# Reading cached value pages four at a time in every second unit, in a one-core decoder-layer kernel

## The chip, the core and the metric

The kernel runs on one core of a Trainium2 chip. The metric is device time in microseconds, from one launch; the median of three runs of the kernel before is 2697.33 us (2696.64 to 2697.48).

## The reference, cut to what matters

One decoder layer is computed for a prompt of 256 tokens and for 8 samples of one token each (264 rows in all), in float32: a half-step FFN, a combined projection into three branches, the gates, an output projection, and a second half-step FFN. Two branches read caches of the samples, and these are what the change is about:

```python
k_past = cache_k[l][page_table].reshape(DB, past_len, A_HEADS, A_DH)   # 8 samples x 8 pages of 128 x 1024 f32
v_past = cache_v[l][page_table].reshape(DB, past_len, A_HEADS, A_DH)
...
o = einsum('bhqsj,bhqsjd->bqhd', p_sel, vs) + einsum('bhqj,bhjd->bqhd', p_own, v_own)   # attention over pages (MoBA)
...
s = einsum('bqhd,bmhd->bhqm', q, mk) * (M_DH ** -0.5)                   # attention over 256 memory tokens
return einsum('bhqm,bmhd->bqhd', softmax(s), mv)
```

A sample has 8 key pages and 8 value pages (512 KB each), and 2 key blocks and 2 value blocks of memory (512 KB each).

## The kernel before, in words

**The main stream.** Every weight matrix goes through TensorE in units. `sp_mid_unit` (SyncE) loads a block of weights into one of four places of `raw` (1 MB, or 512 KB for the short units); ACT copies it rounded into `splitH` (`act_split`, L487), DVE makes the remainder `splitL` (`dve_split`, L493), and PE runs three matmuls for each pair of tiles (`pe_unit`, L533 to L535) against the 264 columns. A long unit has 48 matmuls, a short one 24. The middle of the kernel is one loop of 176 units, T = 0 to 175, that every engine writes out in full. In the stretch of the gates, T = 64 to 127, the units with T % 4 of 0 and 1 are long (gate weights) and those with T % 4 of 2 and 3 are short (branch weights); T = 128 to 143 are long again.

**The side work.** Everything else is hung behind units by number: after unit T, PE runs `pe_side(T)`, ACT runs `act_side(T)` after its split for unit T + 2, and DVE runs `dve_side(T)` after its split for unit T + 2. The prompt's own attention over eight heads is one such side work (`pe_heads` with `KA`): from T = 109 to 132 nearly every unit has a score product, a transposition or an output product of it (T = 130 has none, and T = 108 has none).

**The ring.** Pages of keys and values of both branches pass through five places of 512 KB, `ring` (RING = 5). `uses()` sorts all reads by the unit in which they end, PE's reads ahead of DVE's within a unit; the n-th page of that list takes place n % 5, and so the place of the page five before it. POOL issues the loads in that order (`sp_page`, L1630), each after a wait for `page_used` of its place; `LOAD_AT` sets only where in POOL's program the load stands (about six units behind the use that frees the place), so it is the wait that paces it. Key pages are read by DVE (`dve_half_page`, L1674), half a page at a time; `KEY_AT` says how many halves stand in which unit. At T = 83, 86, 89 and 92 two halves stand: the second of one page and the first of the next. Value pages are read by PE as the moving operand of small matmuls with 8 columns of probabilities as weights:

```python
1974:        s = page_there(pe, ("V", k, g))
1975:        for j in range(4):
1976:            last = nc.tensor.matmul(PS[32 * j:32 * j + A_HEADS, 4, 0:2 * P], DA["L"][:, k, g, :],
...
1978:        last.then_inc(page_used[s], 1)
```

(`pe_value_page`; `pe_mem_values` at L1964 does the same for the two blocks of a sample's memory.) When the eight pages of a sample have been read, ACT copies the PSUM rows out (`act_row_copy`), PE transposes them ahead of the next sample's first page (`pe_row_turn`, L1510), and DVE takes the diagonal out (`dve_past_row_out`).

**The two lists of the change.** `MEM_AT` gives the unit in which each sample's memory values are read, `VALUE_AT` how many value pages each unit reads. The steps of PE, ACT and DVE all follow these lists, and so do the ring's order and POOL's loads. Before, memory values stand in T = 83, 84, 86, 87, 89, 90, 92 and 93, two blocks each; value pages stand in T = 108 to 131 as 3, 2, 1, 2 by T % 4, and two each in T = 132 to 139.

Of the kernel before, what the change touches and what calls it, by code (L numbers as in the profile page):

```python
# [83 lines left out]
def build(nc, d, o, sem, PS, block):  # L84
# [1418 lines left out]
    def pe_row_turn(pe, n):  # L1503

        pe.wait_ge(row_sb, n + 1)
        wait_count(pe, row_out, n)
        if n == MEM_ROWS:
            pe.wait_ge(a_lo, M_HEADS)
        for et in range(2):
            last = nc.tensor.transpose(PS[:, turn_bank(n), et * P:(et + 1) * P], row_tile(n)[:, n % 2, et, :], ident[:, :])  # L1510
        last.then_inc(row_turned, 1)

    def dve_rows_out(dve, n, out):

        dve.wait_ge(row_turned, n + 1)
        for et in range(2):
            rows = PS[:, turn_bank(n), et * P:(et + 1) * P].rearrange("p (h c) -> p h c", h=4)
            last = nc.vector.tensor_copy(out[:, et:BT:2, :], rows[:, :, 0:DEC])
        last.then_inc(row_out, 1)
# [59 lines left out]
    assert sum(KEY_AT.values()) == 2 * len(KEYS)  # L1579
    MEM_AT = (83, 84, 86, 87, 89, 90, 92, 93)  # L1580
    VALUES = [("V", k, g) for k in range(DEC) for g in range(NPAGES)]
    VALUE_AT = {**{T: (3, 2, 1, 2)[T % 4] for T in range(108, 132)}, **{T: 2 for T in range(132, 140)}}
    assert sum(VALUE_AT.values()) == len(VALUES)

    def uses():

        at_slot, n = [], 0
        for T in sorted(KEY_AT):
            for _ in range(KEY_AT[T]):
                n += 1  # L1590
                if n % 2 == 0:
                    at_slot.append((T, 1, KEYS[n // 2 - 1]))
        for b, T in enumerate(MEM_AT):
            at_slot += [(T, 0, ("MV", b, g)) for g in range(2)]
        v = 0
        for T in sorted(VALUE_AT):
            for _ in range(VALUE_AT[T]):
                at_slot.append((T, 0, VALUES[v]))
# [33 lines left out]
    def page_read(eng, page):  # L1632

        n = PAGE_NO[page]
        eng.wait_ge(page_used[n % RING], n // RING + 1)
# [277 lines left out]
    def act_exps(act, K):  # L1913

        act.wait_ge(d_logit, K.q + 1)
        last = nc.scalar.activation(K.t["L"][:, :, :, :], K.t["L"][:, :, :, :], ACT.Exp)
        if K is DKA:
            last = nc.scalar.activation(K.t["eo"][:, :, :], K.t["om"][:, :, :], ACT.Exp)
        last.then_inc(d_exp, 1)
# [16 lines left out]
    def dve_probs(dve, link, K):  # L1936

        t = K.t
        dve.wait_ge(sum_ps, K.q + 1)
        tot = PS[:, sum_bank(K), 2 * P:2 * P + DEC * K.heads].rearrange("p (b h) -> p b h", b=DEC)  # L1940
        if K is DKA:
            link(nc.vector.tensor_tensor(t["rd"][:, :, :], tot, t["eo"][:, :, :], ALU.add))
        else:
            link(nc.vector.tensor_copy(t["rd"][:, :, :], tot))
        link(nc.vector.reciprocal(t["x1"][:, :, :], t["rd"][:, :, :]))
        for g in range(K.pages):
            last = nc.vector.tensor_tensor(t["L"][:, :, g, :], t["L"][:, :, g, :], t["x1"][:, :, :], ALU.mult)
        if K is DKM:
            link(last)
            w = K.pages * K.heads  # L1950
            last = nc.vector.tensor_copy(t["one"][:, :].rearrange("p (b c) -> p b c", b=DEC)[:, :, 0:DEC * w:DEC],
                                         t["L"][:, :, :, :].rearrange("p b g h -> p b (g h)"))
        last.then_inc(d_prob, 1)

    def pe_mem_values(pe, b):

        if b == 0:
            pe.wait_ge(d_prob, 1)
            pe.wait_ge(row_sb, MEM_ROWS)
        for g in range(2):  # L1960
            s = page_there(pe, ("MV", b, g))
            for h in range(M_HEADS):
                c0 = DEC * (M_HEADS * (2 * b + g) + h)
                last = nc.tensor.matmul(PS[32 * h:32 * h + DEC, 4, 0:M_DH], DM["one"][:, c0:c0 + DEC],  # L1964
                                        ring[:, s, h * M_DH:(h + 1) * M_DH], start=b == 0 and g == 0,
                                        stop=b == DEC - 1 and g == 1)
            last.then_inc(page_used[s], 1)
# [132 lines left out]
    def pe_side(pe, T, values):  # L2100
# [24 lines left out]
        for b in range(DEC):  # L2125
            if T == MEM_AT[b]:
                pe_mem_values(pe, b)
        if T == MEM_AT[DEC - 1] + 1:
            pe_row_turn(pe, MEM_ROWS)
# [4 lines left out]
        pe_heads(pe, KA, T, MOBA, 3, 5)  # L2134
        for _ in range(VALUE_AT.get(T, 0)):
            k, g = values // NPAGES, values % NPAGES
# [8 lines left out]
    def pe_heads(pe, K, T, t0, pitch, lag):  # L2145

        for h in range(K.heads):
            t = t0 + pitch * h
            if T == t:
                att_scores(pe, K, h)  # L2150
            if T == t + 4:
                att_turn(pe, K, h)
            if T == t + lag:
                att_out(pe, K, h)
# [12 lines left out]
    def dve_heads(dve, link, K, T, t0, pitch, lag):  # L2167

        for h in range(K.heads):
            t = t0 + pitch * h  # L2170
            if T == t + lag:
                dve_att_lo(dve, K, h)
        for h in range(K.heads):
            t = t0 + pitch * h
            if T == t + 2:
                dve_att_norm(dve, link, K, h)
            if T == t:
                dve_att_soft(dve, K, h)
# [15 lines left out]
    def act_side(act, T, values):  # L2194
# [33 lines left out]
        if T == 79:  # L2228
            act_exps(act, DKM)
        if T == MEM_AT[DEC - 1]:  # L2230
            page_read(act, ("MV", DEC - 1, 1))
            act_row_copy(act, MEM_ROWS)
        act_heads(act, KA, T, MOBA, 3, 5)
        if T == 104:
            act_exps(act, DKA)
        for _ in range(VALUE_AT.get(T, 0)):
            k, g = values // NPAGES, values % NPAGES
# [26 lines left out]
    def dve_side(dve, link, T, keys, values):  # L2264
# [50 lines left out]
        if T == 81:  # L2315
            dve_probs(dve, link, DKM)
        if T == MEM_AT[DEC - 1] + 1:
            dve_rows_out(dve, MEM_ROWS, DM["oS"])
# [16 lines left out]
        dve_heads(dve, link, KA, T, MOBA, 3, 5)  # L2335
        for _ in range(VALUE_AT.get(T, 0)):
            k, g = values // NPAGES, values % NPAGES
# [320 lines left out]
```

## Time and profile before

| what | value |
|---|---|
| median of three runs | 2697.33 us |
| the profiled execution's own time | 2698.35 us |
| its span | 2696.7 us, 50854 instructions |
| PE / PEld busy | 2668.9 us (99%) / 2596.7 us (96%) |
| DVE / ACT / POOL busy | 1541.8 / 1091.3 / 148.2 us (57, 40, 5%) |
| mean granted clock of TensorE | 0.996 |
| moved by DMA | 601.13 MB, mean 223 GB/s; 265 to 393 GB/s in the eight slices from 1146 to 1685 us |
| loads `ring<-cache_v` | 64 of 512 KB, issued by POOL, median 5.6 us to landing |

Busy time is given per engine and overlaps between engines. The chain that ended last is followed backwards from the last instruction to what released each step; the row with the largest part names what the time was spent on. Times inside the trace are from the start of the span. L-numbers are lines of the kernel.

### The profile page before, as it was taken

How to read it: one execution, taken by the hardware profiler on the slowest of the kernel's cores; microseconds unless marked ns; L12 is line 12 of the kernel's file. 1: busy time of each engine (PE TensorE's matmuls, PEld its weight loads, DVE VectorE, ACT ScalarE, POOL GpSimd, SP SyncE). 2: the span in 40 equal slices, each digit the busy share in tenths (PEclk: the TensorE clock that was granted, in tenths of full speed). 3: DMA queues.
4: the chain of work that ended last, by engine and by line, in shares of the span. 5: the costliest groups of instructions: out<-in, count | busy, mean ns of one | idle time of the engine just before them, and what ended most of it. 6: DMA issues, size and time to landing. Idle time of an engine off the chain costs nothing.

```text
span 2696.7 us, 50854 instructions
## 1 busy us (share of the span) xinstructions
PE 2668.9 (99%) x21748; PEld 2596.7 (96%) x21748; DVE 1541.8 (57%) x2441; ACT 1091.3 (40%) x984; POOL 148.2 (5%) x267
## 2 busy tenths in 40 slices
PE   8999999999999999999999999999999999999998
PEld 7899999999999999999998988899999999999998
DVE  4545555555457778876675744365545555455455
ACT  6433333333335433455352444344433333333345
POOL 0000000000000011111211121100000000000000
PEclk9999999999999999999999999999999999999999
DMA  7665555555545799799989799766555555555543
GB/s 265 235 208 175 184 183 177 187 176 183 187 161 175 238 305 299 242 354 393 341 277 348 265 315 322 235 205 199 176 181 177 186 179 182 181 179 186 180 159 115
DMA packets 487721, 601.13 MB, mean 223 GB/s; under 512 B 12624, under 2 KB 447024, under 8 KB 486256
## 3 DMA queue, kind: packets, MB, share of 16 engines
q1 hardware_dynamic: 442512, 456.37, 52.5%
q0 software_dynamic: 35360, 130.79, 13.4%
q10 hardware_dynamic: 9680, 11.54, 1.2%
q8 instruction: 129, 2.11, 0.3%
q14 instruction: 40, 0.33, 0.0%
HBM read 575.16 MB, written 25.58 MB: 223 GB/s over the span
## 4 chain that ended last, share of the span: by engine, by line
PE 96%; DMA 1%; DVE 1%; ACT 1%; issue 1%; DVEq 0%; ACTq 0%; POOLq 0%
PE PS L533 30%; PE PS L534 29%; PE PS L535 29%; PE PS L1976 1%; PE PS L569 1%; PE PS L571 1%; PE PS L570 1%; DVE splitL L493 1%; DMA raw<-w_gate 1%; ACT splitH L487 1%; PE PS L1739 0%; DMA mtok<-mem_prompt 0%; PE PS L1476 0%; PE PS L1707 0%; PE PS L1221 0%
## 5 line engine op out<-in xcount | busy, mean ns | idle before, releaser
L493 DVE TENSOR_TENSOR splitL<-raw,splitH 128x2048 fp32r<-128x2048 f32 (+1 forms) x463 | 1009.9, 2181 | 848.2 <-ACT splitH L487 847.3
L487 ACT ACTIVATE splitH<-raw 128x2048 fp32r<-128x2048 f32 (+1 forms) x463 | 845.6, 1828 | 1499.5 <-PE PS L535 1449.1
L533 PE MATMUL PS<-gH,splitH 128*128 128x264 f32 x3072 | 881.6, 287 | 6.1 <-DVE splitL L493 6.1
L534 PE MATMUL PS<-gL,splitH 128*128 128x264 f32 x3072 | 872.0, 284 | 0.0
L535 PE MATMUL PS<-gH,splitL 128*128 128x264 f32 x3072 | 871.3, 284 | 0.0
L533 PEld LDWEIGHTS PS<-gH,splitH 128*128 128x128 f32 x3072 | 580.0, 189 | 25.8 <-issue 24.8
L534 PEld LDWEIGHTS PS<-gL,splitH 128*128 128x128 f32 x3072 | 580.4, 189 | 0.5 <-issue 0.2
L535 PEld LDWEIGHTS PS<-gH,splitL 128*128 128x128 f32 x3072 | 577.5, 188 | 0.0
L533 PE MATMUL PS<-hH,splitH 128*128 128x264 f32 x1536 | 437.5, 285 | 0.1
L534 PE MATMUL PS<-hL,splitH 128*128 128x264 f32 x1536 | 436.4, 284 | 0.0
L535 PE MATMUL PS<-hH,splitL 128*128 128x264 f32 x1536 | 436.1, 284 | 0.0
L533 PEld LDWEIGHTS PS<-hH,splitH 128*128 128x128 f32 x1536 | 290.6, 189 | 0.4 <-issue 0.3
L534 PEld LDWEIGHTS PS<-hL,splitH 128*128 128x128 f32 x1536 | 290.7, 189 | 0.1
L535 PEld LDWEIGHTS PS<-hH,splitL 128*128 128x128 f32 x1536 | 289.2, 188 | 0.0
L533 PE MATMUL PS<-hidH,splitH 128*128 128x264 f32 x704 | 200.7, 285 | 0.5 <-DVE splitL L493 0.2
L533 PE MATMUL PS<-hid2H,splitH 128*128 128x264 f32 x704 | 200.5, 285 | 0.3 <-DVE splitL L493 0.2
L534 PE MATMUL PS<-hid2L,splitH 128*128 128x264 f32 x704 | 199.6, 283 | 0.0
L534 PE MATMUL PS<-hidL,splitH 128*128 128x264 f32 x704 | 199.6, 283 | 0.0
L535 PE MATMUL PS<-hid2H,splitL 128*128 128x264 f32 x704 | 199.3, 283 | 0.0
L535 PE MATMUL PS<-hidH,splitL 128*128 128x264 f32 x704 | 199.3, 283 | 0.0
L1674 DVE CUSTOM_DVE_ANT_0 ring<-ring,qB 128x128 f32<-128x128 f32 (+1 forms) x560 | 131.9, 298 | 20.1 <-DMA ring<-cache_k 20.0
L533 PEld LDWEIGHTS PS<-hidH,splitH 128*128 128x128 f32 x704 | 132.5, 188 | 2.1 <-issue 1.4
(377 smaller groups left out, 2968.6 us busy)
## 6 DMA issues: line engine op xcount, KB each, us to landing
raw<-ffn_w SPq DMA_DIRECT2D x240, 1024.0 KB, 5.1
raw<-w_in SPq DMA_DIRECT2D x64, 1024.0 KB, 6.8
raw<-w_gate SPq DMA_DIRECT2D x48, 1024.0 KB, 8.1
ring<-cache_k POOLq DMA_DIRECT2D x64, 512.0 KB, 5.7
ring<-cache_v POOLq DMA_DIRECT2D x64, 512.0 KB, 5.6
raw<-ffn_w SPq DMA_DIRECT2D x32, 768.0 KB, 4.8
raw<-w_out SPq DMA_DIRECT2D x16, 1024.0 KB, 5.6
raw<-w_mem_kv SPq DMA_DIRECT2D x15, 1024.0 KB, 6.3
```

Source lines behind the costliest of these rows:

```text
L487: nc.scalar.activation(splitH[:, s, tiles, :], raw[:, u, 0:nk, :], ACT.Copy).then_inc(hi_ready, 1)
L493: nc.vector.tensor_tensor(splitL[:, s, tiles, :], raw[:, u, 0:nk, :], splitH[:, s, tiles, :].bitcast(F32), ALU.subtract).then_inc(split_re ...
L533: nc.tensor.matmul(out, w_hi, H[:, k, 0:n], start=first, stop=False)
L534: nc.tensor.matmul(out, w_hi, L[:, k, 0:n], start=False, stop=False)
L535: last = nc.tensor.matmul(out, w_lo, H[:, k, 0:n], start=False, stop=final)
L569: nc.tensor.matmul(out, t_hi, w_hi, start=u == 0 and j == 0, stop=False)
L570: nc.tensor.matmul(out, t_hi, w_lo, start=False, stop=False)
L571: last = nc.tensor.matmul(out, t_lo, w_hi, start=False, stop=u == 3 and j == 3)
L1674: last = nc.vector.tensor_tensor_reduce(k, k, query(Q_SLOT[j])[:, h * w:(h + 1) * w], 1.0, 0.0, ALU.mult, ALU.add, S[:, b, g, h:h + 1])
L1976: last = nc.tensor.matmul(PS[32 * j:32 * j + A_HEADS, 4, 0:2 * P], DA["L"][:, k, g, :], ring[:, s, 2 * j * P:2 * (j + 1) * P], start=g == ...
```

## The change

Only the two lists change.

```diff
-    MEM_AT = (83, 84, 86, 87, 89, 90, 92, 93)
+    MEM_AT = (84, 84, 87, 87, 90, 90, 93, 93)
     VALUES = [("V", k, g) for k in range(DEC) for g in range(NPAGES)]
-    VALUE_AT = {**{T: (3, 2, 1, 2)[T % 4] for T in range(108, 132)}, **{T: 2 for T in range(132, 140)}}
+    VALUE_AT = {T: 4 for T in range(109, 141, 2)}
     assert sum(VALUE_AT.values()) == len(VALUES)
```

Memory values of two samples, four blocks, are read together at T = 84, 87, 90 and 93. Value pages are read four at a time at T = 109, 111, ... 139. Every block and page is still read once, in the same order among the values; because `uses()` sorts by unit, the order of key and value pages in the ring changes between T = 83 and 93.

## Rows read from the trace of the kernel before

**Rows 1.** The page: the chain that ended last, by engine.

```profile
PE 96%; DMA 1%; DVE 1%; ACT 1%; issue 1%; DVEq 0%; ACTq 0%; POOLq 0%
```

**Rows 2.** Windows: start:end, length, engines' busy us, PEclk, DMA share, GB/s.

```profile
1450.00:1457.60 7.60, 4.51 (x45) 3.55 (x43) 3.31 (x12) 1.91 (x1) 1.05 (x2) 1.00 1.02 390
1457.60:1465.20 7.60, 7.60 (x52) 7.46 (x56) 4.35 (x18) 0.00 (x0) 0.53 (x1) 0.78 0.90 305
...
1536.00:1650.00 114.00, 114.00 (x1048) 98.28 (x1047) 52.60 (x85) 56.25 (x90) 26.16 (x49) 1.00 0.91 311
```

**Rows 3.** Chain of waits, 1410 to 1480: total us, times, longest.

```profile
DVE ring L1674 <- DMA ring<-cache_k: 20.0, 6, 6.9
...
PE PS L533 <- DVE splitL L493: 3.1, 1, 3.1
```

**Rows 4.** Chain that ended last, memory values: start, us, what.

```profile
1412.55 0.98 PE PS L1964 x16
...
1419.53 0.98 PE PS L1964 x16
...
1433.52 0.98 PE PS L1964 x16
...
1446.30 0.59 PE PS L1964 x8
...
1448.09 6.17 DMA ring<-cache_k
```

**Rows 5.** The same chain, value pages.

```profile
1548.47 0.98 PE PS L1976 x16
1552.88 0.55 PE PS L1976 x8
...
1557.21 0.98 PE PS L1976 x16
```

**Rows 6.** PE's timeline: start, us, engine, line; transpositions alone, then before pages.

```profile
1476.05 0.38 PE L1510 MATMUL PS<-ident_s,orow 128*128 128x128 f32 x2
1476.19 0.37 PE L533 MATMUL PS<-orH,splitH 128*128 128x264 f32 x1
...
1564.67 0.38 PE L1510 MATMUL PS<-ident_s,orow 128*128 128x128 f32 x2
1564.98 1.48 PE L1976 MATMUL PS<-ring,A_L 128*8 128x256 f32 x24
```

**Rows 7.** POOL's timeline: page loads behind the pages read at 1548.47.

```profile
1550.49 0.53 POOL L1630 DMA_DIRECT2D ring<-cache_v  x1 [5.17 <-PE PS L1976]
1551.66 0.53 POOL L1630 DMA_DIRECT2D ring<-cache_v  x1 [0.64 <-issue]
```

**Rows 8.** Page loads of L1630 in 1548:1558, then in 1645.8:1655.4, then in 1397:1500.

```profile
DMA to landing us min/median/max: 3.9/5.2/7.2
...
DMA to landing us min/median/max: 5.5/7.7/7.7
...
DMA to landing us min/median/max: 3.5/6.7/10.1
```

**Rows 9.** DVE's timeline, memory stretch; in brackets the idle time before.

```profile
1431.44 0.29 DVE L1674 CUSTOM_DVE_ANT_0 ring<-ring,qB 128x128 f32<-128x128 f32 x1
...
1436.33 0.29 DVE L1674 CUSTOM_DVE_ANT_0 ring<-ring,qB 128x128 f32<-128x128 f32 x1 [3.96 <-DMA ring<-cache_k]
...
1437.19 0.70 DVE L2024 TENSOR_TENSOR accT<-EV,PS 128x528 f32<-128x528 f32 x1
1437.81 2.28 DVE L493 TENSOR_TENSOR splitL<-raw,splitH 128x2048 fp32r<-128x2048 f32 x1
...
1454.29 0.29 DVE L1674 CUSTOM_DVE_ANT_0 ring<-ring,qB 128x128 f32<-128x128 f32 x1 [6.92 <-DMA ring<-cache_k]
...
1470.92 0.29 DVE L1674 CUSTOM_DVE_ANT_0 ring<-ring,qB 128x128 f32<-128x128 f32 x1 [2.50 <-DMA ring<-cache_k]
...
1475.40 2.29 DVE L493 TENSOR_TENSOR splitL<-raw,splitH 128x2048 fp32r<-128x2048 f32 x1 [0.52 <-ACT splitH L487]
```

**Rows 10.** PE's timeline: the first matmul of unit 96.

```profile
1479.19 0.28 PE L533 MATMUL PS<-gH,splitH 128*128 128x264 f32 x1
```

## The prediction, made before the changed kernel was run

> **What bounds the kernel now.** I read the page first. TensorE holds 96% of the chain that ended last [rows 1], so time is won only by giving PE less to do or fewer pauses, and anything that makes PE wait is paid in full. Next I read windows over the two stretches that the change touches. From 1536 to 1650 us, where value pages are read, PE is busy throughout at full clock, but the DMA engines are busy 0.91 of the time at 311 GB/s [rows 2]: PE is the bound and the queues are the next thing behind it. In the memory stretch the waits show 20.0 us in six waits of DVE for key pages, and one PE wait of 3.1 us for a split that DVE made late [rows 3]. The chain shows its cause: the page whose place PE freed at 1446.30 is issued at 1448.09 and takes 6.17 us [rows 4]. Behind that pause the granted clock is 0.78 over 7.6 us where it was 1.00 [rows 2], so part of it was at the lower level, 1.2 GHz. I price that as (1 - 0.78) x 7.6 = 1.7 us.
>
> **The size of the gain.** The work in the matmuls does not change, so what can be saved is the fixed cost of entering and leaving a group. A one-page group takes 0.55 us and a two-page group 0.98 [rows 5]: 0.43 us a page and 0.12 over. The entry comes from spacings. From 1412.55 to 1419.53 is one long unit and one two-block group, 6.98 us; from 1433.52 to 1446.30 are two equal halves more of unit work (a long unit and two halves, 96 matmuls) and one group, 12.78 us [rows 4]. Their difference gives 5.80 us for 48 matmuls, and 6.98 - 5.80 - 0.98 = 0.20 us remains outside the group. A group alone therefore costs 0.32 us beyond its pages.
>
> The change removes 4 groups of memory values (T = 83, 86, 89, 92) and 16 of value pages (every even T from 108 to 138). Most of these 16 stand beside a product or a transposition of the prompt's attention, which could have paid the entry anyway. Two row transpositions alone reach the next unit after 0.14 us; the same two ahead of pages take 0.31 us to the first page [rows 6]. So a joined group costs 0.17 more at its entry and 0.12 at its end, 0.29 us. I use 0.32 for all, as the two are nearly equal. If joined groups were free, 5 value groups (T = 108, 130, 134, 136, 138) would be left, so the bounds for value pages are 5 x 0.32 = 1.6 and 16 x 0.32 = 5.1 us; I take **-5.1**, since rows 6 show the joined case. The row transpositions move from even to odd units and stay joined to a group; their number does not change. ACT's row copies still follow pages 7 of each sample at T % 4 = 3, and now have two units until the next sample instead of one. The transposition's copy on DVE stands one unit later, behind its split, and the next split is needed about 10 us later: no cost while DVE has that much. POOL's bias loads for a head queue behind up to four page loads, some 2.3 us later than now at 1.16 us a load (below), under the 6 us at least that a head's unit needs; no cost.
>
> **Pages in the short pairs.** The ring has five places. With four freed at once, the next group needs the spare page and three reloads. Where two long units lie between the groups there are 13 us or more. In five places only two short units do: T = 109 to 111, 113 to 115, 117 to 119, 121 to 123 and 125 to 127. There the group starts were 8.74 us apart [rows 5]; a one-page group goes (0.43 + 0.32) and two pages come (0.87), which gives 8.86 us. The fourth page of the next group is wanted after three more pages, at +8.86 + 1.30 = +10.2 us. Its load is the third: POOL starts the first at 1550.49 - 1548.47 = +2.0 us and the next 1.16 later [rows 7], so the third at +4.3. It may take 5.9 us to land without a wait. Loads in such a window took 5.2 us by the median, 7.2 at most; in the last such window 7.7 [rows 8]. The third would land at +9.5, +11.5 or +12.0, waits of 0, 1.3 and 1.8 us. A fourth load now shares the engines, which were at 311 GB/s already. I take 0.5 us a window, nearer to the median, so **+2.5** for five; bounds are 0, and with the 10.1 us seen in the memory stretch [rows 8] 4.2 each, 21 us.
>
> The Trainium skill speaks against this part: "DMA: Bandwidth & Descriptors", section Bandwidth, gives 6.15 us for a 1 MB transfer. As an estimate by that page, three reloads of 512 KB need 9.2 us from the first start, landing at +11.2 and waiting 1.0 us a window, which would make this term 5.0 and not 2.5. The trace shows more than that page's 341 GB/s, 390 in one window [rows 2], so I leave the term as it is.
>
> **Keys between the memory values.** Here the order of the ring changes. Written out by unit it becomes K(83) MMMM(84) K(84) K(86) MMMM(87) K(87) K(89) MMMM(90) K(90) K(92) MMMM(93) K(93). At T = 83, 86, 89 and 92 DVE reads the second half of one key page and then the first of the next. That next page is now five behind the first, so its load can only start when DVE has finished that half. Before, the place was a memory block's that PE had freed. The waits there were 3.96 at T = 86, 6.92 at T = 89 and 2.50 at T = 92 [rows 9].
>
> T = 86: the second half starts at 1431.44 and takes 0.86 (1436.33 to 1437.19) [rows 9]; with 1.1 us for POOL (from its second load's spacing) and the 6.7 us median of this stretch [rows 8] the page is there at 1440.1, against 1436.33. The first half, the accumulation of 0.62 and the split of 2.28 [rows 9] end at 1443.9, where the split ended at 1440.09: PE waits some 3.6 us for unit 89, and the clock may fall, 1.7 more. T = 89: the second half ends near 1448.9, the page lands near 1456.1, against 1454.29 [rows 9]. So unit 92 starts 1.8 us later than now, and the loss of T = 86 is inside this, because the pause that stands there now is filled by it. The three group savings before unit 92 are inside it too. In return the 1.7 us of lower clock behind the old pause fall away. T = 92 and 93: the page for T = 93 takes the place of the first block read at T = 93, freed near 1471.9, issued at 1473.0 and landing near 1477.7 (4.7 in quieter queues). Half a page and a split of 2.29 [rows 9] end at 1480.9. Unit 96 starts at 1479.19 now [rows 10]: 1.7 us late, and perhaps a lower clock, for which I put half, 0.8. Together +1.8 - 1.7 - 0.3 (the group at T = 92) + 1.7 + 0.8 = **+2.3** for this stretch. From below it is -1.3, the four groups and no new wait; from above, landings of 10.1 us at the last wait (+3.4) and two falls of clock (+3.4) give +9.
>
> Sum: -5.1 + 2.5 + 2.3 = -0.3 us on the profiled execution's 2698.35, whose span is 2696.7; the median of the runs lies 1.0 lower than that execution, at 2697.33. Forecast 2697.0 us. About 0.2%, 5.4 us, is what a measurement can tell from no change.
>
> **Rivals.**
> - *Slower, page waits in the short pairs.* If the third reload lands after 8.3 us, each window waits 2.4 us, 12 in all in place of 2.5: 2706.5. It decides from 7.6 us on, where the sum passes +5.4. For it: 7.7 in the last window, the DMA share of 0.91. Against: 5.2 in the first, and raw weight loads are thin between the short units. 0.15.
> - *Slower, key waits in the memory stretch.* Four waits of DVE on pages that it must free itself, with landings of 10.1 and the clock falling twice, give +9 in place of +2.3: 2703.7. For it: DVE's 20.0 us of waits now. Against: DVE's slack and the old pause, which swallows the first loss. 0.12.
> - *Faster, all waits hidden.* Pages land within 5.9 us in the short pairs and the key reloads land in 5, their competition being thinner at these times. Then only the groups count, 20 x 0.32 = 6.4: 2690.9. For it: medians of 5.2. Against: the circular wait above, which has no slack at T = 89. 0.21.
> - *The change does not do what it says.* The lists' sums are kept, 64 pages and 8 samples, and every engine follows them, so this would need groups to be split again by another side step. 0.02, no change in time.
>
> **How the numbers follow.** The forecast has 0.50 and with the last rival gives no change 0.52. Slower is 0.15 + 0.12 = 0.27, faster 0.21. Gains and losses of five microseconds each nearly cancel, so the middle is likeliest though neither term is sure. The range runs from the hidden case, 2690.5, to the page waits, 2706.5, and leaves out the far tail above and a little below.
>
> **What would show it.** In the value stretch: groups of four pages of 0.12 + 4 x 0.43 = 1.84 us, 16 of them; even units with none; long units 13.7 us apart in pairs from T = 133 on. PE waits for `ring<-cache_v` of about 0.5 us in the short pairs; none or over 2 us each prove the term wrong. In the memory stretch: DVE waits for `ring<-cache_k` of 5 to 8 us at four units, more than 30 us in total where there were 20.0; a PE pause of 3 us ahead of unit 89 in place of the one ahead of unit 92; a short one ahead of unit 96. The forecast is wrong if the spacing of the value groups shows that joined groups cost nothing, or if PE's pauses between 1410 and 1490 sum to over 8 us.

## The result, and the profile after

The changed kernel takes 2700.88 us by the median of 20 runs (2697.46 to 2707.03), the kernel before 2697.23 us over 20 runs beside them: +3.65 us, a ratio of 1.0015 with a 95% interval of 1.0009 to 1.0021, that is 2.4 to 5.7 us. (A ratio in this document is formed from all runs of both kernels and is not the quotient of the two medians, so the two can differ by 0.1%.) The difference is inside the 5.4 us that I called no change, and the time is inside the range; but the forecast was 0.3 us faster, and the kernel is slower, by little and clear of the noise of these runs.

The profiled execution of the changed kernel happens to be the quickest of its 20 (2697.46 us, span 2695.8), quicker than the profiled one of before (2698.35). The spans alone would mislead, so I compare stages. PE's timeline gives fixed points in both: the sum over `M_se` (T = 81), the sum over `own` (T = 99), the sum over `A_se` (T = 106) and the last row transposition (T = 140). After the change:

```profile
1401.92 0.30 PE L1933 MATMUL PS<-M_se,ones 128*128 128x32 f32 x2
...
1494.95 0.43 PE L1834 MATMUL PS<-own,ones 128*128 128x64 f32 x2
...
1532.00 0.33 PE L1933 MATMUL PS<-A_se,ones 128*128 128x64 f32 x2
...
1747.42 0.38 PE L1510 MATMUL PS<-ident_s,orow 128*128 128x128 f32 x2
```

The same four before the change:

```profile
1404.60 0.30 PE L1933 MATMUL PS<-M_se,ones 128*128 128x32 f32 x2
...
1496.87 0.43 PE L1834 MATMUL PS<-own,ones 128*128 128x64 f32 x2
...
1530.64 0.33 PE L1933 MATMUL PS<-A_se,ones 128*128 128x64 f32 x2
...
1748.72 0.38 PE L1510 MATMUL PS<-ident_s,orow 128*128 128x128 f32 x2
```

Differences of neighbours: the memory stretch 92.3 us before and 93.0 after, the stretch from T = 99 to 106 33.8 and 37.0, the value stretch 218.1 and 215.4. The first time was 2.7 us earlier after the change, in code that is the same in both; that is the spread between executions, and it is why single spans cannot be compared here.

The chain that ended last, by engine, has PE at 92% where it had 96% [rows 1]; DMA and DVE took what it lost:

```profile
PE 92%; DMA 3%; DVE 2%; ACT 1%; issue 1%; POOLq 0%; SPq 0%; DVEq 0%; POOL 0%; ACTq 0%
```

**Memory stretch.** The waits from 1400 to 1500 us, to be compared with [rows 3]:

```profile
DVE ring L1674 <- DMA ring<-cache_k: 26.7, 4, 7.8
...
PE PS L533 <- DVE splitL L493: 5.7, 4, 2.0
```

DVE's timeline gives the four waits one by one; before there were six, three of which stand in [rows 9]:

```profile
1421.25 0.29 DVE L1674 CUSTOM_DVE_ANT_0 ring<-ring,qB 128x128 f32<-128x128 f32 x1 [6.19 <-DMA ring<-cache_k]
...
1435.58 0.29 DVE L1674 CUSTOM_DVE_ANT_0 ring<-ring,qB 128x128 f32<-128x128 f32 x1 [6.21 <-DMA ring<-cache_k]
...
1451.99 0.29 DVE L1674 CUSTOM_DVE_ANT_0 ring<-ring,qB 128x128 f32<-128x128 f32 x1 [7.83 <-DMA ring<-cache_k]
...
1471.07 0.29 DVE L1674 CUSTOM_DVE_ANT_0 ring<-ring,qB 128x128 f32<-128x128 f32 x1 [6.47 <-DMA ring<-cache_k]
```

These are T = 83, 86, 89 and 92, where DVE reads the second half of one page and then the first half of the page that takes its place. T = 93, 96 and 97 hold such a pair of halves too, but their pages take places that PE freed, and DVE did not wait there. PE's pauses that follow are four short ones (2.04, 1.94, 0.91 and 0.81 us, ahead of units 89, 92, 95 and 96) in place of one of 3.09 ahead of unit 92.

**T = 99 to 106.** This stage I had not priced. The chain that ended last, as its longest pieces (start, us, what), runs through one weight load:

```profile
1480.94 17.66 DMA raw<-w_gate
1498.62 1.93 ACT splitH L487
1500.58 2.29 DVE splitL L493
1502.87 0.54 DVE A_gate L1845 x4
```

ACT's timeline shows the wait for it:

```profile
1498.62 1.92 ACT L487 ACTIVATE splitH<-raw 128x2048 fp32r<-128x2048 f32 x1 [6.90 <-DMA raw<-w_gate]
```

and PE's timeline shows two pauses behind it:

```profile
1502.92 0.39 PE L533 MATMUL PS<-gH,splitH 128*128 128x264 f32 x1 [0.82 <-DVE splitL L493]
...
1517.43 0.36 PE L533 MATMUL PS<-gH,splitH 128*128 128x264 f32 x1 [2.55 <-DVE splitL L493]
```

The load of a gate weight took 17.7 us, ACT waited 6.90 of them, DVE's split came late, and DVE's long chain of gates, comparisons and logits behind it (T = 99 to 101) came late too, so that its later split held PE for 2.55 us. Before the change ACT waited for no load between 1478 and 1525 us, and PE's longest pause in this stage was 0.42 us.

**Value stretch.** Groups of four pages are there as foretold, 1.84 us each in the chain:

```profile
1573.31 1.84 PE PS L1976 x32
...
1582.48 1.84 PE PS L1976 x32
...
1597.33 1.84 PE PS L1976 x32
```

and in two of the five short pairs the fourth page was late:

```profile
1559.70 0.62 PE L1976 MATMUL PS<-ring,A_L 128*8 128x256 f32 x8 [1.21 <-DMA ring<-cache_v]
...
1632.47 0.62 PE L1976 MATMUL PS<-ring,A_L 128*8 128x256 f32 x8 [0.76 <-DMA ring<-cache_v]
```

### The profile page after: what moved, and what is told of

It reads as the page before. It is cut to its first block, busy times and chain, and to the rows that moved or that the text cites. A ratio compares the mean times of both kernels' runs of the same rounds, so it can differ in the third digit from the quotient of the medians.

```text
span 2695.8 us, 50854 instructions
## 1 busy us (share of the span) xinstructions
PE 2660.3 (99%) x21748; PEld 2594.3 (96%) x21748; DVE 1541.5 (57%) x2441; ACT 1092.9 (41%) x984; POOL 148.2 (5%) x267
## 4 chain that ended last, share of the span: by engine, by line
PE 92%; DMA 3%; DVE 2%; ACT 1%; issue 1%; POOLq 0%; SPq 0%; DVEq 0%; POOL 0%; ACTq 0%
PE PS L533 29%; PE PS L534 28%; PE PS L535 28%; DVE splitL L493 2%; DMA raw<-w_gate 1%; PE PS L1976 1%; PE PS L569 1%; PE PS L571 1%; PE PS L570 1%; ACT splitH L487 1%; DMA ring<-cache_k 1%; DMA ring<-cache_v 1%; DMA raw<-w_mem_kv 1%; PE PS L1739 0%; PE PS L1707 0%
## 5 line engine op out<-in xcount | busy, mean ns | idle before, releaser
L1674 DVE CUSTOM_DVE_ANT_0 ring<-ring,qB 128x128 f32<-128x128 f32 (+1 forms) x560 | 131.9, 300 | 26.7 <-DMA ring<-cache_k 26.7
```

The lines of the kernel that those rows point to most:

```text
L1674: last = nc.vector.tensor_tensor_reduce(k, k, query(Q_SLOT[j])[:, h * w:(h + 1) * w], 1.0, 0.0, ALU.mult, ALU.add, S[:, b, g, h:h + 1])
```

## The experiments

Each kernel was timed in 6 to 11 runs against the kernel before on the same chip. The medians of before were 2697.61 us for the first four kernels below (one half at a time, even units, whole keys with memory values in fours), 2696.67 for the changed kernel once more and for the last one, and 2697.43 for the other four. A difference in us is one of medians. The table of stages at the end of this section takes PE's times at the fixed points above.

**One half of the change at a time.** First the memory values alone:

```diff
-    MEM_AT = (83, 84, 86, 87, 89, 90, 92, 93)
+    MEM_AT = (84, 84, 87, 87, 90, 90, 93, 93)
```

> Memory values as changed, value pages as before. Theory A (the loss is DVE's wait for a key page whose place it frees itself just before, at T = 83, 86, 89 and 92): slower than before by 3 to 7 us; DVE's waits for ring<-cache_k between 1400 and 1500 us come in four, 25 us or more in sum, and PE pauses for splits ahead of units 86 to 96. Theory B (the loss is in the value stretch, where four loads burst into two short units): within 2 us of before, since the four groups saved (4 x 0.32 = 1.3 us) and the waits cancel.

Measured 2703.21 us, +5.6, ratio 1.0017 (1.0008 to 1.0026). DVE waited 28.9 us in four waits. Theory A holds against theory B, but more than its own stretch is in the number: the stage from T = 99 to 106 took 37.7 us here too, and what that cost theory A does not explain. Then the value pages alone:

```diff
-    VALUE_AT = {**{T: (3, 2, 1, 2)[T % 4] for T in range(108, 132)}, **{T: 2 for T in range(132, 140)}}
+    VALUE_AT = {T: 4 for T in range(109, 141, 2)}
```

> Value pages as changed, memory values as before. Theory A: faster than before by 1.5 to 4 us (16 groups less at 0.32 us, 5.1, less page waits of some 2.5 us in the five short pairs). Theory B: slower by 2 to 6 us, with PE waiting over 8 us in sum for ring<-cache_v. Theory C (a group that stands beside another side product costs nothing extra, so only 5 groups count): 1.6 us less and 2.5 us more, within 1.5 us of before.

Measured 2695.24 us, -2.4, ratio 0.9991 (0.9982 to 1.0000). Theory B falls: this half alone does not lose. From theory C it is not told apart by the time alone; the next run does that.

**The same groups without the short pair.**

```diff
-    VALUE_AT = {T: 4 for T in range(109, 141, 2)}
+    VALUE_AT = {T: 4 for T in range(108, 140, 2)}
```

> Four value pages at every even unit from 108 to 138, so that each gap between groups in the gates holds one long and one short unit, some 12 us, in place of 9 and 16 in turn; memory values as before. The number of groups is that of the change. Theory A: no PE wait for ring<-cache_v at all, and faster than before by 4 to 6 us, the 16 groups in full. Theory C: faster by 1.6 us or less, though nothing waits. Theory B, if it is the burst of loads as such that delays the weights: slower than before, with ACT waiting for raw.

Measured 2689.98 us, -7.6, ratio 0.9970 (0.9959 to 0.9981). PE's waits for `ring<-cache_v` are gone, and the value stretch took 212.9 us, 5.2 less than before, which over 16 groups is 0.32 us for each, joined or alone; theory C falls. The whole time fell by 2.4 us more than this stage, which no stage accounts for; the interval, 5.1 to 11 us, reaches down to the stage's own number.

**Whole key pages.** DVE reads the two halves of a page in one unit. Every second page still takes the place of the one read just before it (that order is set by the memory values), but it is wanted two units later and no longer in the same unit:

```diff
-              76: 1, 77: 1, 78: 1, 79: 2, 80: 2, 81: 1, 82: 1, 83: 2, 84: 1, 85: 1, 86: 2, 87: 1, 88: 1, 89: 2,
-              90: 1, 91: 1, 92: 2, 93: 2, 94: 1, 95: 1, 96: 2, 97: 2, 98: 1}
+              76: 1, 77: 1, 78: 1, 79: 2, 80: 2, 81: 1, 82: 1, 83: 1, 85: 2, 86: 2, 88: 2, 89: 2,
+              91: 2, 92: 2, 94: 2, 95: 2, 96: 2, 97: 2, 98: 2}
```

With memory values in fours and value pages as before:

> Memory values as changed, and the key pages from T = 84 on read as whole pages (two halves of one page in one unit, at T = 85, 86, 88, 89, 91, 92, 94 to 98), so that no page's load waits for the page read just before it in the same unit; value pages as before. Theory A: the four long key waits go, DVE waits less than 8 us for ring<-cache_k there, PE has no pause of over 1 us between units 83 and 96, and the time is 4 to 7 us below before (the old pause of 3.1 us with its lower clock, 1.7, and four groups, 1.3). Rival: the waits come from the engines of the DMA being full (0.92 busy), so that key pages come as late as before and the time is within 2 us of the kernel with the memory values changed alone.

Measured 2693.55 us, -4.1, ratio 0.9986 (0.9977 to 0.9995). Its waits in the same stretch:

```profile
PEld PS L1964 <- DMA ring<-cache_mem_v: 2.4, 2, 2.1
...
DVE ring L1674 <- DMA ring<-cache_k: 2.3, 1, 2.3
...
PE PS L1964 <- DMA ring<-cache_mem_v: 1.6, 1, 1.6
```

DVE's waits, 28.9 us with the memory values changed alone, have become 2.3 with the DMA engines no less full (0.95 busy from 1405 to 1480 us, against 0.90 there), so the rival (the queues themselves are late) falls. One part of the expectation missed: PE now has a pause, 1.6 us, for the fourth memory block. With memory values in pairs, as before, and whole key pages alone:

> Memory values and value pages as before; only the key pages from T = 84 on are read whole. Theory A: the page waits of the kernel before (20.0 us of DVE, one PE pause of 3.1 us with a lower clock behind it) were of the same kind, since there too the first half of a page was wanted in the unit that freed its place; 3 to 6 us faster than before, so that most of what the kernel with whole key pages and memory values in fours gained is due to the keys, and the fours themselves give 1.3 us. Rival: pairs of memory values need the halves as they were, and waits of PE for ring<-cache_mem_v take their place: no faster than before.

Measured 2693.88 us, -3.6, ratio 0.9990 (0.9981 to 0.9999), with no DVE wait for a key page and one of 1.3 us on PE for a memory block. So most of the 4.1 us came from the keys. For the grouping of the memory values by four the expectation was 1.3 us; the stage is 1.0 us shorter with it (88.7 against 89.7 us), which the whole times cannot resolve.

**The burst behind the late weight load.** POOL's burst (biases, `qaR`, `kaR`, value pages) begins 0.6 us behind a 1 MB gate load in both kernels, with its two 1 MB copies 3.3 us behind it. What the change moves is the gate load before that one. Each of the two is issued at the end of a DVE split (1477.04 and 1480.91 us after the change), and the late splits lie closer together. SyncE's timeline after the change; the row merges two issues of 0.37 us, so they start 3.86 us apart:

```profile
1477.07 4.23 SPq L371 DMA_DIRECT2D raw<-w_gate  x2
```

The copies follow in POOL's timeline:

```profile
1484.23 0.54 POOL L2442 DMA_DIRECT2D qaR<-scratch_qaT  x1
1484.76 0.54 POOL L2443 DMA_DIRECT2D kaR<-scratch_kaT  x1
```

The gate loads before the change, 5.99 us apart:

```profile
1477.72 6.36 SPq L371 DMA_DIRECT2D raw<-w_gate  x2
```

The experiment keeps the changed kernel and moves the two copies out of the burst; the biases stay:

```diff
-        if T == 102:
+        if T == 104:
             pool.wait_ge(unit_used, 8 * (B_GATE + 4))
             pool.wait_ge(qa_kept, 32)
             pool.wait_ge(k_sent, 48)
             pool.dma_start(qaR[:, :, :].rearrange("p a c -> p (a c)"), scratch["qaT"]).then_inc(qk_in, 16)
             pool.dma_start(kaR[:, :, :].rearrange("p a c -> p (a c)"), scratch["kaT"]).then_inc(qk_in, 16)
```

> The changed kernel with POOL's two 1 MB loads qaR and kaR moved from T = 102 to T = 104 in POOL's program, behind two more page loads. In the changed kernel's trace ACT waited 6.9 us for a weight load that took 17.7 us to land, and PE paused 2.6 us ahead of a later unit; before the change that load took 9.6. Theory D (the late key pages push two gate loads together, 3.9 us apart in place of 6.0, and into the burst of POOL's eight loads): the load lands in 11 us or less, the pause between T = 99 and T = 106 goes, and the time is 2 to 4 us below the changed kernel's, near 2697.5. Rival: the pause comes from DVE's chain of gates and logits, which starts late behind the split, whatever the copies do: within 1 us of the changed kernel.

Measured 2697.96 us, ratio to the kernel before 1.0007 (0.9998 to 1.0016), 2.9 us below the changed kernel. The issues of the gate loads are 3.86 us apart as they were:

```profile
1480.53 4.23 SPq L371 DMA_DIRECT2D raw<-w_gate  x2
```

but the second load landed, by the view of the loads of `raw` issued from 1484 to 1485 us, in

```profile
DMA to landing us min/median/max: 10.2/10.2/10.2
```

and the stage took 33.8 us, as before the change. In these profiles the late load needs both circumstances. With the copies behind it and the gate loads 6.0 us apart it landed in 9.6 us before the change and in 5.4 to 12.0 in six more kernels; with the loads 3.9 us apart and the copies 10 us later it landed in 10.2, in one profile; with both it took 17.7, 18.3 and 18.7 in three profiles. The rival falls, since in the kernel with the copies moved DVE's splits in the memory stretch are late as well (its DVE waits are 28.8 us), its chain of gates is the same, and the pause is gone.

**The changed kernel once more, for the spread.**

> The changed kernel once more, for a second profile, to see how much its memory stretch varies. By stages, from the sum over M_se (T = 81) to the one over own (T = 99), from there to the sum over A_se (T = 106), from there to the last row transposition (T = 140): the sum of theories A and D asks for 93 to 97, 37 to 38 and 215 to 216.5 us, with the weight load behind the burst at 15 us or more. If the middle stage is back at 34, the late weight load was chance and does not explain the loss.

Measured 2699.96 us, ratio 1.0012 (1.0003 to 1.0021). The late load was no chance: 18.7 us. The middle stage took 39.6 us, above the 37 to 38 that were expected and 2.6 more than in the first profile. Of these, 1.0 is the first of the two pauses, 1.85 us where it was 0.82; the rest is the clock. The second pause, ahead of the same unit, is 2.55 us in the first profile and 2.56 in this one. The 8 us behind it, as windows (PEclk stands third from the right), are in the first profile

```profile
1517.40:1525.40 8.00, 7.97 (x66) 8.00 (x67) 6.13 (x16) 1.82 (x2) 0.28 (x1) 1.00 0.80 262
```

and in the second, for the pause of 2.56 us and for one of 2.67 in the memory stretch,

```profile
1521.60:1529.60 8.00, 8.00 (x53) 8.00 (x54) 5.36 (x15) 0.31 (x1) 0.24 (x1) 0.79 0.80 261
...
1442.90:1450.90 8.00, 7.95 (x53) 7.95 (x54) 4.82 (x27) 0.29 (x1) 1.06 (x2) 0.79 0.98 300
```

The granted clock was 0.79, so part of each window at 1.2 GHz: 53 matmuls where 66 fitted, 0.21 x 8 = 1.7 us lost each time. The same pause of 2.55 us left the clock at 1.00 in the profile with the memory values changed alone too, so it was paid once in three. The span is 2703.0 us, 7.2 above the first profile's; 2.6 of these lie in the middle stage and 2.6 ahead of T = 81, in code that is the same.

Read in the same way, the pauses and the clock behind them account for most of the spread of the memory stretch, which the table at the end shows. Behind the longest pause of each memory stretch the granted clock over 8 us was 1.00 (2.04 us of pause, the changed kernel), 0.79 (2.67, the same kernel again; 2.98, value pages alone; 3.09, before), 0.82 (3.42, memory values alone), 0.63 (3.71, even units) and 0.64 (3.96, copies later). The last two as windows, even units first:

```profile
1456.31:1464.31 8.00, 8.00 (x44) 8.00 (x45) 4.37 (x18) 0.00 (x0) 0.53 (x1) 0.63 0.87 291
...
1442.32:1450.32 8.00, 8.00 (x44) 8.00 (x45) 4.77 (x26) 0.00 (x0) 1.06 (x2) 0.64 0.93 302
```

The share missing from 1.00, times 8 us, is the loss: 0 to 3.0 us. Taking it and PE's pauses of 0.4 us and more from the seven stages leaves 87.1 to 87.9 us, where the stages themselves run from 92.3 to 96.2.

**Both repairs.** Memory values in fours, whole key pages, value pages at even units:

> Memory values in fours as changed, key pages whole from T = 84 on, value pages four at every even unit. The two stretches lie apart, so their gains should add: 4.1 + 7.6 = 11.7 us below before, 2686; bounds 8 to 13 us. A sum much below 8 would mean that both gains were the same pause.

Measured 2688.72 us, -8.7, ratio 0.9976 (0.9966 to 0.9985). The stages gain 3.4 and 5.2 us, 8.6, as the medians do; by the ratio's interval the gain is 4 to 9 us, so that my 11.7 is missed and the lower bound of 8 is not sure. The 11.7 had added medians, of which the even units' 7.6 held 2.4 us that belong to no stage. With the copies at T = 104 as well:

> As the kernel with both repairs, and the copies qaR and kaR at T = 104 as well. Theory D: that kernel has no such pause (its gate loads are 6.0 us apart), so this moves nothing, within 1 us of it. Rival: the burst costs something in every kernel, and this is 2 us faster.

Measured 2687.87 us, ratio 0.9967 (0.9955 to 0.9979); 0.9 us from the run above, not told apart from it. Theory D asked for that: where the two gate loads keep their distance, no harm of the copies can be seen. And with memory values left in pairs:

> Whole key pages and value pages in fours at even units, with memory values in pairs as before the change. The kernels with whole keys took 2693.9 with memory values in pairs and 2693.6 in fours. Theory A: the same difference here, so 1 us above the kernel with both repairs at most, 2689 to 2690; rival: fours bring page waits of PE that pairs do not have, and this is 1 to 2 us faster, 2687.

Measured 2687.67 us, ratio 0.9970 (0.9959 to 0.9980), 9.0 us below its kernel before. This expectation is not decided: the time alone is the rival's 2687, but this chip's kernel before was 0.8 us quicker as well, and the stage T = 81 to 99 is 0.7 us longer than with fours (89.6 against 88.9), as theory A has it. The three best kernels lie within 1.1 us, which these runs do not separate. The simplest of them is the last: key pages whole from T = 84 on, the value pages in fours at even units, the memory values not touched.

Stages in us, from PE's timeline of each profile:

| kernel | T = 81 to 99 | T = 99 to 106 | T = 106 to 140 |
|---|---|---|---|
| before | 92.3 | 33.8 | 218.1 |
| changed, two profiles | 93.0; 93.6 | 37.0; 39.6 | 215.4; 215.9 |
| memory values alone | 95.0 | 37.7 | 218.1 |
| value pages alone | 93.1 | 33.8 | 215.9 |
| value pages, even units | 94.6 | 33.8 | 212.9 |
| whole keys, memory in fours | 88.7 | 33.8 | 218.1 |
| whole keys alone | 89.7 | 33.8 | 218.1 |
| changed, copies later | 96.2 | 33.8 | 215.7 |
| both repairs | 88.9 | 33.8 | 212.9 |
| both repairs, copies later | 89.0 | 33.8 | 212.9 |
| both, memory in pairs | 89.6 | 33.8 | 212.9 |

The two right columns repeat to 0.1 us wherever nothing waits, and the four value stretches with short pairs to 0.5. The left one varies by 2 to 3 us for the same code: 92.3, 93.1 and 94.6 with memory values and keys as before, 93.0, 93.6, 95.0 and 96.2 with the change; the pauses and the clock behind them make that spread.

## Why the prediction was wrong, point by point

**The groups: right.** -5.1 us was forecast for 16 groups of value pages; the even units, where no page is waited for, gave -5.2. That joined groups cost as much as lone ones, read from the transpositions [rows 6], is confirmed.

**Pages in the short pairs: right.** +2.5 us forecast; 215.4 to 215.9 in four profiles against 212.9 without short pairs is 2.5 to 3.0. It was spread otherwise than written: in the profile two of the five windows wait visibly for the fourth page, 1.2 and 0.8 us on PE, and one shows no pause but a longer group (2.00 us where the others have 1.91). The estimate worked out from the 6.15 us that the Trainium skill, "DMA: Bandwidth & Descriptors", section Bandwidth, gives for 1 MB was 5.0 us; these profiles show half of that.

**Keys between the memory values: mechanism right, size near.** +2.3 us forecast. By the left column, the mean of four with the change is 94.5 and of three without it 93.3: +1.1 us, with a spread in each group of two to three times that, so the term's size is not settled; +2.3 looks too high. The circular waits are where they were foretold, 6.2, 6.2, 7.8 and 6.5 us on DVE; the sum of 26.7 (26.7 to 28.9 in the four profiles with the change) fell short of "more than 30". The pause ahead of unit 89, forecast as 3.6 us, was 2.0, 2.7, 3.4 and 4.0 in these four, and the one ahead of unit 92, which I let vanish, was 1.9, 0.5, 0.6 and gone. Ahead of unit 96 stood 0.8 us instead of 1.7, and one of 0.4 to 1.1 ahead of unit 95 had no place in the sum. The clock fell behind the pause at unit 89 in three of the four; the sum had reckoned that loss as hidden, and had put the chance of one behind unit 96 at one half, where it never came. A small misreading changes no term: the 1446.30 given as the time at which PE freed a place is the start of that read, which ends at 1446.89.

**What failed** is a term that the sum did not have. The part on POOL's burst said of the side work only that loads queue "under the 6 us at least that a head's unit needs; no cost", and the part on keys ended at unit 96. I did not ask what the late splits do to SyncE: a weight load is issued when DVE has finished with its place, so splits that come late and then close together issue loads close together, and here right ahead of 2 MB of copies. The sum put this stage at nothing, for the reason that a head's unit leaves 6 us, which speaks of another load. It cost 37.0, 37.7 and 39.6 against 33.8 us, a mean of +4.3. With the parts above, +1.1 + 4.3 - 2.4 = +3.0, beside the measured +3.65 (2.4 to 5.7). Without it the forecast would have stood as far as runs can tell: the kernel with the copies moved is at a ratio of 1.0007, and its interval includes 1. Some luck is in that, because by the stages' mean the key term was 1.2 us too high.

The rival that was nearest was the one of key waits in the memory stretch, with 2703.7 us and a chance of 0.12; DVE's four waits are where the loss begins, as it says, but what it priced (landings of 10.1 us and a clock that falls twice, in the memory stretch) is not what cost the most; that lay one stage later. The size stayed within the 0.2% that was called the likeliest outcome. Part of that is luck too: with the missing term of +4.3 us and the other terms as forecast, the sum is +4.0, near the edge of 5.4.

## What to carry to other kernels

In a ring whose places are handed on in order, write down for each load which read frees its place and how far that read stands ahead of the next use; here half a page read at the end and the first half of the page that takes its place wanted right behind it cost DVE a wait of 6.0 to 8.5 us each time, nearly a full load's time to landing. Leaving two units between the two was worth 3.6 us even in the kernel before (0.3 to 5.1 by its interval), where PE freed the place in the unit in which DVE wanted the page. When side work is gathered into larger groups, put the groups where the gaps between them are equal, since the shortest gap sets the waits and the count of groups sets the gain. And follow a delay on one engine to the transfers that it releases, up to the next burst of another queue.

## What the runs showed of the hardware

A 1 MB weight load took 17.7 to 18.7 us to land when it was issued 3.9 us behind another and 3.3 us ahead of two 1 MB copies of POOL. It took 5.4 to 12.0 us with the other load 6.0 us ahead and the copies 3.3 to 4.0 behind, in seven profiles, and 10.2 with the copies 10 us behind, in one. Pauses of PE of 2.55 and 2.56 us ahead of the same unit left the granted clock at 1.00 in two executions and at 0.79 over 8 us in a third, a difference of 1.7 us for the same pause; behind pauses of 3.71 and 3.96 us it was 0.63 and 0.64 over 8 us. A small group of 8-column matmuls within the stream of 128-column ones cost 0.32 us beyond its own matmuls, an average over 16 of them.
